# A hybrid decoder step on one core: ten cache copies issued by Pool ahead of the query weights, six under way on the sync queue

## What is computed

```python
h = rms_norm(x) * (1 + scale) + shift               # modulation from c @ w_ada
qa,ka,va,qb,kb,vb = h @ w_in                        # two groups of 8 heads
oa = stick_breaking(qa, paged cache sb_k/sb_v + new)       # 2048 past keys per sample
ob = dilated_attention(qb, window cache dil_k/dil_v + new) # windows 128/1, 512/4, 2048/16
x = x + gate * (concat(norm(oa), norm(ob)) @ w_out)
# PEER: q = h2 @ w_peer_q, scores against sub keys, top 16 of 16384 experts per head
x = x + gate2 * sum_k weight_k * peer_v[expert_k]   # weight_k from gelu(peer_u[expert_k] . h2)
outputs: rms_norm(x), the new keys and values, and
dil_k_sample, dil_v_sample = window buffers shifted by one row, new row at the end
```

## Time and profile before

| what | us |
|---|---|
| median of 3 runs | 1211.17 |
| lowest, highest | 1208.58, 1219.85 |
| the profiled execution | 1215.47 |
| its span | 1213.8 |

### The profile page before, as it was taken

One profiled execution on the slowest core, in us unless ns is written; L12 is line 12 of the kernel. 1 busy time (PEld: TensorE's weight loads), 2 busy tenths in 40 slices (PEclk: granted clock), 3 DMA queues, 4 the chain that ended last, 5 costly groups with the idle time before them and its releaser, 6 DMA issues.

```text
span 1213.8 us, 13371 instructions
## 1 busy us (share of the span) xinstructions
PE 909.9 (75%) x3662; PEld 423.6 (35%) x3662; DVE 635.5 (52%) x1604; ACT 351.8 (29%) x959; POOL 420.2 (35%) x430
## 2 busy tenths in 40 slices
PE   2797986668676879964778877877587777777783
PEld 0342443445232448831323322333233322323231
DVE  4200106553222544223776777777777777777755
ACT  0000001463121012221333233323433444244323
POOL 1201323112231000211455554545454455555551
PEclk9799988777898889977999999999999999999996
DMA  9999999988999899999999999999989999999996
GB/s 366 424 379 400 378 365 364 397 338 351 373 392 413 281 367 378 388 396 393 410 414 428 420 428 427 428 428 428 428 357 427 428 427 428 428 428 428 427 427 272
DMA packets 72826, 481.21 MB, mean 396 GB/s; under 512 B 9953, under 2 KB 10306, under 8 KB 27346
## 3 DMA queue, kind: packets, MB, share of 16 engines
q0 software_dynamic: 54720, 377.53, 76.0%
q1 hardware_dynamic: 18066, 103.17, 22.1%
HBM read 477.41 MB, written 70.32 MB: 451 GB/s over the span
## 4 chain that ended last, share of the span: by engine, by line
DMA 46%; PE 30%; issue 8%; DVE 8%; ACT 3%; POOL 2%; SPq 2%; POOLq 0%; DVEq 0%; ACTq 0%
DMA R<-in_uv,idst 29%; PE ps L968 11%; DMA out_dil_v_s<-in_dil_v 6%; DMA R<-in_sb_v,vrow 5%; PE ps L919 5%; PE ps L874 2%; PE ps L576 2%; POOL R L480 2%; DMA R<-in_sb_k 2%; DVE R L1770 2%; DMA vrow<-in_vrow 2%; PE ps L739 2%; PE ps L602 1%; DMA R<-in_uv,idec 1%; ACT wgt L1241 1%
## 5 line engine op out<-in xcount | busy, mean ns | idle before, releaser
L968 PE MATMUL ps<-R,diag 128*128 128x512 f32 x1024 | 491.9, 630 | 168.8 <-ACT diag L1260 167.3
L480 POOL DMA_INDIRECT R<-in_uv,idst x256 | 313.7, 1225 | 365.6 <-PE ps L968 294.6
L1770 DVE CUSTOM_DVE_ANT_0 R<-R,H 128x1024 f32<-128x1024 f32 x264 | 319.3, 1224 | 201.7 <-DMA R<-in_uv,idst 190.7
L968 PEld LDWEIGHTS ps<-R,diag 128*128 128x128 f32 x1024 | 195.7, 199 | 465.0 <-ACT diag L1260 252.0
L1238 ACT ACTIVATE gel<-dots 128x2 f32<-128x2 f32 x132 | 26.8, 203 | 403.9 <-DVE dots L1770 403.9
L576 PE MATMUL ps<-R,HT 128*128 128x512 f32 x192 | 94.3, 631 | 3.9 <-DMA R<-in_wts 3.9
L1260 ACT ACTIVATE diag<-const,wgt 128x128 f32<-128x128 f32 x256 | 88.9, 394 | 14.7 <-PE ps L968 1.4
L310 POOL DMA_INDIRECT R<-in_sb_v,vrow x32 | 30.4, 951 | 114.5 <-PE ps L739 90.2
L432 POOL DMA_DIRECT2D R<-in_wts x24 | 12.8, 541 | 157.3 <-PE ps L874 57.2
L301 POOL DMA_DIRECT2D R<-in_sb_k x64 | 34.7, 542 | 86.5 <-issue 85.9
L1241 ACT ACTIVATE wgt<-gel,gst 128x1 f32<-128x1 f32 x264 | 63.3, 287 | 4.3
(11 more groups left out here) (282 smaller groups left out, 828.6 us busy)
## 6 DMA issues: line engine op xcount, KB each, us to landing
R<-in_wts POOLq DMA_DIRECT2D x48, 1024.0 KB, 17.0
out_dil_k_s<-in_dil_k SPq DMA_DIRECT2D x32, 1023.5 KB
out_dil_v_s<-in_dil_v SPq DMA_DIRECT2D x32, 1023.5 KB
R<-in_sb_k SPq DMA_DIRECT2D x64, 256.0 KB, 8.3
R<-in_sb_k POOLq DMA_DIRECT2D x64, 256.0 KB, 6.7
R<-in_win_v SPq DMA_DIRECT2D x8, 512.0 KB
R<-in_uv,idst POOLq DMA_INDIRECT x256, 11.8
m_all<-in_win_k SPq DMA_DIRECT2D x6, 512.0 KB
```

Source lines behind the costliest of these rows:

```text
L480: pool.indirect_dma_start(out=R[:, row_slot(k), :], out_offset=None, in_=A["uv"], in_offset=bass.IndirectOffsetOnAxis(ap=idst[:, par, k:k ...
L968: last = pe.matmul(ps[:, banks + q, :], diag[:, k % 4, :], R[:, row_slot(k), D + q * 512:D + (q + 1) * 512], start=False, stop=False, skip ...
L1770: dve.tensor_tensor_reduce(u, u, H[:, t, :], 1.0, 0.0, ALU.mult, ALU.add, dots[:, k:k + 1]).then_inc(s["dot_done"], 1)
```

## The change

The copies get a running number n from 0 to 63, with the sample n // 8, the quarter of the buffer and the buffer (key or value). SP keeps six under way, on six semaphores in turn: copy n waits for copy n - 6. Sixteen stay where they were; ten (16 to 25) now stand before the dilated value rows of sample 2, where four stood; Pool issues ten (26 to 35) without a wait behind its last value gather and ahead of the query weights; SP issues the remaining 28 where 44 stood.

```diff
+COPIES = 8 * NB
+EARLY, POOL_FROM, POOL_COPIES, SP_AHEAD = 16, 26, 10, 6
...
-        copied = [sem(f"copied{n}") for n in range(4)]
+        copied = [sem(f"copied{n}") for n in range(SP_AHEAD)]
...
+        def copy_piece(eng, n):
+
+            b, q, m = n // 8, n % 8 // 2, n % 2
+            src, dst = ((A["dil_k"], A["dil_k_s"]), (A["dil_v"], A["dil_v_s"]))[m]
+            size = (PAST - 1) * DG // 4
+            return eng.dma_start(dst[b:b + 1, q * size:(q + 1) * size].rearrange("a (r n) -> (a r) n", r=P),
+                                 src[b:b + 1, q * size + DG:(q + 1) * size + DG].rearrange("a (r n) -> (a r) n", r=P))
...
-                landed = copied[2 * odd + m]
-                if not (isinstance(pair, int) and isinstance(q, int) and pair + q == 0):
-                    sp.wait_ge(landed, pair * 64 + q * 16)
...
+            def copies(first, end):
+
+                for n in range(first, end):
+                    landed = copied[n % SP_AHEAD]
+                    if n >= SP_AHEAD:
+                        sp.wait_ge(landed, 16 * (n // SP_AHEAD))
+                    copy_piece(sp, n if n < POOL_FROM else n + POOL_COPIES).then_inc(landed, 16)
...
-            for odd in range(2):
-                copy_windows(0, odd)
+            copies(0, EARLY)
...
                 if b == 2:
-                    copy_windows(1, 0, range(2))
+                    copies(EARLY, POOL_FROM)
...
-            copy_windows(1, 0, range(2, 4))
-            for pair, odd in ((1, 1), (2, 0), (2, 1), (3, 0), (3, 1)):
-                copy_windows(pair, odd)
+            copies(POOL_FROM, COPIES - POOL_COPIES)
...
+            sp.wait_ge(s["copied_pool"], 16 * POOL_COPIES)
...
+            for n in range(POOL_FROM, POOL_FROM + POOL_COPIES):
+                copy_piece(pool, n).then_inc(s["copied_pool"], 16)
             weight_rounds(10, CHUNKS // WSLOTS)
```

More of the change, by code:

```diff
@@ L254, in build @@
           diag_done e_used ff_ready f_rt y_ready y_out hr_mm hr_ev idec_ready dve act dst dis tks subk_in
-          z_v topsm tope fin_in""".split()
+          z_v topsm tope fin_in copied_pool""".split()
         s = {n: sem(n) for n in names}
@@ L329, in _ @@
             sp.wait_ge(s["pages_in"], 32)
-            def copy_piece(pair, odd, m, q):
-                src, dst = ((A["dil_k"], A["dil_k_s"]), (A["dil_v"], A["dil_v_s"]))[m]
-                n = (PAST - 1) * DG // 4
-                landed = copied[2 * odd + m]
-                if not (isinstance(pair, int) and isinstance(q, int) and pair + q == 0):
-                    sp.wait_ge(landed, pair * 64 + q * 16)
[L339 to L346, removed]
+            def copies(first, end):
[4 more added lines that the diff above has]
+                    copy_piece(sp, n if n < POOL_FROM else n + POOL_COPIES).then_inc(landed, 16)
             sp.wait_ge(s["w_used"], 4)
             key_pages(sp, 0, EVEN, first=True)
-            for odd in range(2):
-                copy_windows(0, odd)
+            copies(0, EARLY)
             with sp.Fori(1, 4) as b:
@@ L416, in _ @@
             sp.wait_ge(s["new_v"], 32)
-            for n in range(4):
-                sp.wait_ge(copied[n], 16 * 4 * NB // 2)
+            for n in range(SP_AHEAD):
+                sp.wait_ge(copied[n], 16 * len(range(n, COPIES - POOL_COPIES, SP_AHEAD)))
+            sp.wait_ge(s["copied_pool"], 16 * POOL_COPIES)
             sp.wait_ge(s["y_out"], 16 * (2 + QUADS))
```

## The result

| kernel | median us | ratio to before, with 95% interval |
|---|---|---|
| before | 1210.76 (4 runs, the three shown before and one more) | 1 |
| changed | 1234.77 (4 runs) | 1.0182 (1.0126 to 1.0239) |

The interval of the ratio is what counts; the quotient of the two medians would be 1.0198. A second measurement of the same changed kernel, on another chip, gave 1.0243 (1.0215 to 1.0272), so ratios from different chips can't be told apart when they differ by 0.6% or less. The profiled execution has a span of 1233.1 us, 19.3 us above that of before. Bytes and packets are the same to the last digit (481.21 MB).

What follows compares the result with a forecast made beforehand. The prediction took transfers to lead (DMA 46% of the chain, PE 30%). Its sum, 0 + 6 us with part 2's 8 us inside the 6, gave 1221.5 us profiled and 1217 us on the median; range 1197 to 1234.

Steps and rivals of the forecast that it cites:

- deeper starvation: Rival, 18%: six under way cut Pool to 49 GB/s, a query weight takes 21 us; +20 us, 1231 us.
- Idle time of 13.7 us: Transfers idle at 262 to 266, 277 to 282 and 398 to 431 us; about the most the change can win.
- Part 1: Sixteen early copies, six under way: sixth and seventh projection weights late, key pages sooner; taken as 0, bounds -2 and +9 us.
- Part 2: Ten copies instead of four before the third sample's rows: attention 8 us later at 398, bounds 6.7 and 10.1.
- Part 3: Pool's ten copies and SP's 28: fourth query weight lands at about 517.5, stage ends at 563 us instead of 523.3.
- One to one between the two queues of copies: Before the query weights, Pool's and SP's 64 KB packets alternate equally, so Pool's ten copies are through at 460 us.
- What the expert stage makes of it: Eight gathers lie ready, so the full expert stream starts at 572.6 us against 567: about +6 us.
- Fair shares: Rival, 24%: Pool gets half of 390 GB/s whatever SP holds, a weight takes 5.4 us; -13 us, 1198 us.
- the early copies alone: Rival, 8%: the projection weights' 9 us are never made up, the rest comes as forecast; +15 us, 1226 us.

## Why the prediction was right, and where it was off

The mechanism was forecast: idle time is filled, a full SP queue keeps Pool's weights waiting, and new idle time opens behind the last copy. The size was not. The forecast was 1217 us, a loss of 0.5%, and "within 1%" was given the most; measured were 1234.8 us and 1.8%, clearly outside of that. The time even lies 0.8 us above the end of the stated range (1234). That it came so near is luck: this end was set by the rival of deeper starvation, whose reason the runs refute. The sum had +6 us, the span of the profiled executions has +19.3, and the medians differ by 24.0 (the profiled execution of before lay 4.7 us above its median). Step by step:

- **Idle time of 13.7 us, and that it can be won.** Right: with two under way all of it is filled. Wrong in that 13.7 us is about the most that can be won. With two under way and both moves the time is 10 us (ratio) to 13 us (medians) lower, but the profiled span is 19.8 us lower. The sum of packet time is no constant: it was 1186.1 us there, 1193.5 before and 1201.9 in the changed kernel, with the same bytes.
- **Part 1, taken as 0, bounds -2 to +9.** This is the largest error. The first value gather moved from 217.44 to 224.43: +7.0 us. The lateness was forecast for the sixth and seventh weight; it came one weight earlier. PE waited 7.98 us for the fifth, which was to "still make it", and 4.95 us for the sixth. The kernel before had one wait of 7.4 us for key pages there, which is gone, so PE's waits from 40 to 130 us grew by 6 us net. The step that failed is the sentence that a full share means that bytes are only reordered. From 60 to 110 us, at a share of 0.96, Pool moved 4.60 MB where it had moved 6.48, and SP hardly more (12.97, before 12.58) in more of the engines' time (69.4%, before 62.2%). Afterwards PE was the bound (35.00 us busy of 35 from 110 to 145), transfers waited for it, and the share fell to 0.89, which is 3.9 us of idle time.
- **Part 2, +8 us.** Right: 13.9 - 7.0 = 6.9 us, in the bounds of 6.7 and 10.1.
- **Part 3.** Right in mechanism, and two errors of size that partly cancel. The term was +31.7 us from the end of attention to the end of the stage, and 50.7 - 13.9 = 36.8 were measured. Up to the fourth query weight less was lost than forecast: 517.85 - 395.53 = 122.3 us behind the last value gather, before 477.73 - 381.62 = 96.1, so +26.2 where the forecast has +31.8. Its 517.5 for this weight (its own terms, 460 and four times 14.1, give 516.4) was met only because attention ended 5.9 us later than it said. Behind the fourth weight the forecast went on at the old pace (45.6 us), as if the copies had gone by 521. They moved until 534, the fifth weight was late too (16.4 us behind the fourth and not 8.4), and PE took 56.2 us to the end of the stage, 10.6 too many. Pool's share was mis-sized a little: 74 GB/s came from one stretch of 9.8 us with four under way, and 67 is the measured rate over 50 us, 15.7 us a weight for 14.1. The clock had no term at all. The matmuls of four of the five chunks behind a wait took 9.1 to 10.4 us at a granted clock of 0.71 to 0.81; that behind the second took 7.39 at 1.00, and all later ones took 7.29.
- **One to one between the two queues of copies.** Not quite. SP's sub keys (8 KB packets) stood in front of its copies and took 21.0 us from issue to landing, 6.8 before, since here it was Pool's queue that held the 64 KB packets. Pool's last copy was issued at 400.87 and landed 53.2 us later, at 454, where 460 was forecast, although attention ended later than forecast.
- **What the expert stage makes of it.** Right in kind: with the eight gathers ready and the copies gone, 50.7 us at the stage's end became 19.3 at the end of the program, 31.4 given back. The forecast gave back 33.7.
- **The rivals.** Fair shares fell (67 of 367 GB/s). Deeper starvation had nearly the right time, 1231, for a wrong reason: its proportion to the number under way fell with the step from two to three. The case of the early copies alone had the right mechanism; it was given 8% and a zero in the sum, and 7.0 of its 9 us were there.

The errors add up: +7.0 for part 1, -1.1 for part 2, +5.1 for part 3, +2.3 for the expert stage, 13.3 us over the 6 of the sum.

The Trainium skill's rule that each DMA engine goes round between its queues a packet at a time (DMA: Bandwidth & Descriptors, "Queues, rings and completion order") agrees with the direction: 64 KB against 8 KB gave Pool 67 GB/s of 367, 16 KB against 8 KB gave it 156 of 395. Turns of equal bytes would have given it half in both. But strictly one packet of the profile each would have given it a ninth and a third, and 18% and 40% were measured. Whether a turn by that rule is one packet of the profile, no run here shows.

## What to carry to other kernels

A transfer that nobody waits for is not free when it runs beside one that an engine does wait for. Here, with packets of 64 KB, two under way acted as a throttle, and taking it off starved the other queue wherever the copies stood. To fill idle time, move the bytes to where the idle time is, and test the number under way as a change of its own. And a DMA share near 1 says neither whose bytes are moved nor how fast. Before calling a stage bound by transfers, see how late the transfer is that PE waits for, and compare the packets' time for the same bytes.

## What the runs showed of the hardware

- Pool's rate beside SP's copies is a step and not a slope: 145 GB/s with two under way, then 72, 66 and 67 with three, four and six (470 to 520 us).
- So is the copies' own cost: 178.4 to 178.9 us of the 16 engines with two under way, 190 to 194 with three or more, for the same packets.
- The share follows the size of the packets: four transfers of 256 KB (16 KB packets) in place of one of 1 MB (64 KB) gave the other queue 156 GB/s and not 67, with the same number of pieces under way, but not in proportion (1.3 and 1.8 packets of Pool for one of the copies).
- The price of small packets is the rate of copies alone: 287 GB/s with 16 KB, 328 with 64 KB, at a full share.
- It works in both directions. The 1 MB load of the sub keys on SP (8 KB packets) took 19.9 to 22.2 us in the nine profiled executions with Pool's copies in 64 KB packets, 12.5 in the one with them in 16 KB packets, and 6.5 to 6.9 in the four without copies on Pool.
